# A residual kept in SBUF: selection matmuls in place of scatters in a top-4-of-32 expert layer

## The chip, the core and the metric

The kernel runs on one core of a Trainium2 chip. The metric is the device time of one execution in microseconds. A core has five instruction streams that run beside each other and meet at semaphores: TensorE (PE, matmuls; its weight loads are PEld), VectorE (DVE), ScalarE (ACT), GpSimd (POOL) and SyncE (SP, which here only issues transfers). Sixteen DMA engines move data between HBM (DRAM) and SBUF; matmul results land in PSUM, eight banks of 512 float32 per partition.

## The reference

One decoder block over 512 tokens of width 1024, in float32: a gated recurrence and a dilated attention share one input and one output projection, then a mixture of 32 experts follows, of which each token uses 4.

```python
def _moe(h, router_w, router_b, w_up, b_up, w_down, b_down):
    logits = (h @ router_w + router_b).astype(jnp.float32)
    top_vals, top_idx = lax.top_k(logits, TOP_K)
    gates = jax.nn.softmax(top_vals, axis=-1)
...
    def expert_block(args):
        xb, e = args
        u = xb @ w_up[e] + b_up[e]
        return _clamped_swiglu(u) @ w_down[e] + b_down[e]
...
    return jnp.zeros((N, D), h.dtype).at[sorted_tok].add(y)
```

The block's output is `_rmsnorm(x + _moe(...), final_norm_g)`. The weights of one expert are 8 MiB up (1024 x 2048) and 4 MiB down (1024 x 1024). The 2048 (token, expert) pairs give an expert 64 tokens on average; by the router's logits for these inputs the counts run from 38 to 92.

## The kernel before

**Stages.** The input projection, recurrence and attention take the first 270 us; the output projection and the router run to 307 us. There the rows x (the residual, tile `X`) are complete in SBUF. They are written to the DRAM tensor `residual_rows`, and the normed rows to `normed_rows`. From 318 us the 32 experts follow, one step each, and then the final norm.

**An expert's step.** An expert gets a block of slots, in groups of 32 rows: three groups (96 slots, `BIG`) or two (64 slots, `LESS`). Before the experts start, the kernel ranks them by their counts on the chip, so that the fuller ones get the large blocks; places 0, 1 and the odd ones are `BIG`, 17 in all. Tokens beyond a block go to further blocks at the end, in a loop that tests at run time whether there are any; with these inputs there are none, and each engine only runs through the tests (`TURNS`).

In step p TensorE computes the up products of expert p and the down products of expert p-1. A weight chunk holds 128 rows of w_up or 256 of w_down, 1 MiB; a step has 8 up chunks and 4 down chunks. The stationary operand is a 128x32 piece of the tokens' columns, so four matmuls with different column groups of the array run at a time, each with 512 (up) or 256 (down) moving columns of the float32 weights. Around the chunks stand small things: bias products (L1746, L1764), eight transposes of the next expert's gathered rows (`x_transposed`, L1720), and four or six transposes of the activation output (`a_transposed`, L1728). Each write to PSUM banks 6 and 7 (tile `T`) is copied out by VectorE.

**Weights.** SyncE loads them in pairs of chunks (2 MiB, `load_pair`) into ten buffers in a fixed order; a load waits for `chunk_used`, that is, for the pair that was in its buffer ten pairs before.

**Rows.** GpSimd gathers the next expert's normed rows by an indirect DMA. When the down products of expert q are complete in banks 4 and 5, ScalarE scales one half of the columns by the gates and VectorE the other (`gated`, L783 and L1376, 32x256 pieces) into `y_rows`, and GpSimd scatters these rows with an adding indirect DMA into `residual_rows` (L588). At the end `residual_rows` is read back into SBUF for the final norm (L553).

**Order.** Everything is written out by hand. The steps 2 to 31 are a loop of three rounds with a body of ten steps (`BODY`, L1816), on each engine.

## Time and profile before

| | |
|---|---|
| Time of three runs, median (lowest to highest) | 1394.54 us (1393.95 to 1395.07) |
| The profiled execution | 1393.91 us, its span 1392.1 us |
| TensorE matmuls busy | 1262.6 us, 91% of the span |
| VectorE, ScalarE, GpSimd busy | 400.2, 277.8 and 102.4 us |
| Bytes moved by DMA | 459.38 MB, 330 GB/s over the span |

A row of a timeline gives start and length in us from the span's start, the engine, the line of the kernel, what is written and read, how many instructions are merged, and in brackets the idle time ahead of it and what ended it. A float32 matmul stands as two records, so "x8" on L1754 is four matmuls. Ends of matmuls are modelled and overlap the next; for a price, starts are subtracted.

### The profile page before, as it was taken

The page shows a single profiled execution, that of the slowest core. Times are in us where ns is not written, and L with a number is a line of the kernel's source. Part 1 is how long each engine was busy: PE and PEld are TensorE (multiplying, and loading weights), DVE is VectorE, ACT ScalarE, POOL GpSimd, SP SyncE. Part 2 cuts the span into 40 slices and gives each one's busy share as a digit, 9 for nine tenths or more (in the row PEclk, how much of TensorE's full clock was granted, in tenths as well). Part 3 has the DMA queues.
Part 4 walks back from the last instruction along what each step waited for, and adds up shares of the span by engine and source line. Part 5 has one row for each costly group of instructions (what it writes and reads, how often), then busy time and mean ns, then how long its engine had stood idle before and what let it go on. Part 6 is the DMA issues. An engine that isn't in the chain of part 4 may idle for free.

```text
span 1392.1 us, 31318 instructions
## 1 busy us (share of the span) xinstructions
PE 1262.6 (91%) x13185; PEld 645.4 (46%) x13186; DVE 400.2 (29%) x854; ACT 277.8 (20%) x553; POOL 102.4 (7%) x140
## 2 busy tenths in 40 slices
PE   7999989999999999999898979897989898998990
PEld 6888866684443443433343434343434343333340
DVE  5766745573221122111111111111112121111115
ACT  6455334321111112111111111110101011111112
POOL 0000001000010011000000000001000010100000
PEclk9999999989999999999999999999999999999995
DMA  8422145259999999999999999999999999999943
GB/s 249 135 70 82 46 178 246 92 222 404 361 395 392 402 391 398 393 395 402 403 402 407 402 406 405 402 403 401 403 405 403 396 401 404 398 413 391 414 155 135
DMA packets 71107, 459.38 MB, mean 330 GB/s; under 512 B 7013, under 2 KB 35845, under 8 KB 46304
## 3 DMA queue, kind: packets, MB, share of 16 engines
q1 hardware_dynamic: 64688, 438.52, 78.6%
q0 software_dynamic: 6288, 18.86, 5.8%
q8 instruction: 113, 1.85, 0.5%
q14 instruction: 18, 0.15, 0.0%
HBM read 442.04 MB, written 17.96 MB: 330 GB/s over the span
## 4 chain that ended last, share of the span: by engine, by line
PE 53%; DMA 42%; DVE 3%; issue 1%; ACT 0%; DVEq 0%; SPq 0%
DMA w_raw_pair<-w_down 41%; PE psum L1754 15%; PE psum L1774 15%; PE psum L1496 8%; PE psum L1493 3%; PE psum L1582 2%; PE psum L1720 2%; PE psum L1630 2%; PE psum L1606 1%; PE psum L1746 1%; PE psum L1800 1%; PE psum L1569 1%; PE psum L1647 1%; PE psum L1458 1%; DMA shape_consts<-shape_constants 0%
## 5 line engine op out<-in xcount | busy, mean ns | idle before, releaser
L1754 PE MATMUL psum<-w_raw_pair,x_slots 128*32 128x512 f32 x5184 | 590.8, 608 | 49.9 <-DMA w_raw_pair<-w_up 49.9
L1754 PEld LDWEIGHTS psum<-w_raw_pair,x_slots 128*32 128x32 f32 x5184 | 165.5, 112 | 432.9 <-issue 356.1
L1774 PE MATMUL psum<-w_raw_pair,a_slots 128*32 128x256 f32 x5184 | 294.0, 381 | 9.6 <-DMA w_raw_pair<-w_down 9.5
L1774 PEld LDWEIGHTS psum<-w_raw_pair,a_slots 128*32 128x32 f32 x5184 | 163.7, 110 | 117.5 <-DMA w_raw_pair<-w_down 13.0
L1363 DVE TENSOR_SCALAR lin<-lin 128x768 f32<-128x768 f32 (+1 forms) x32 | 15.9, 498 | 466.7 <-ACT lin L773 466.6
L773 ACT ACTIVATE lin<-psum 128x768 f32<-128x768 f32 (+1 forms) x32 | 22.8, 711 | 600.2 <-PE psum L1754 600.2
L1376 DVE TENSOR_SCALAR y_rows<-psum,gate_t 32x256 f32<-32x256 f32 x162 | 78.5, 484 | 200.5 <-PE psum L1774 198.6
L783 ACT ACTIVATE y_rows<-psum,gate_t 32x256 f32<-32x256 f32 x162 | 75.5, 466 | 300.0 <-PE psum L1774 298.4
L588 POOL DMA_INDIRECT residual_rows<-y_rows,scatter_rows x32 | 46.4, 1450 | 250.8 <-DVE y_rows L1376 231.1
L1496 PE MATMUL psum<-h_low,w_in_high 128*128 128x512 f32 x160 | 63.9, 399 | 0.0
L1496 PE MATMUL psum<-h_high,w_in_high 128*128 128x512 f32 x160 | 62.6, 391 | 0.0
L1496 PE MATMUL psum<-h_high,w_in_low 128*128 128x512 f32 x160 | 62.5, 391 | 0.0
L1357 DVE TENSOR_SCALAR a_slots<-psum 128x768 f32<-128x768 f32 (+1 forms) x32 | 26.6, 833 | 113.5 <-PE psum L1728 112.4
L576 POOL COPY gather_rows<-row_t 96x1 int32 x32 | 5.8, 182 | 665.3 <-PE psum L1720 643.7
L1353 DVE COPY x_slots<-psum 128x768 f32<-128x768 f32 (+1 forms) x32 | 26.4, 825 | 65.1 <-PE psum L1720 53.5
L1720 PEld LDWEIGHTS psum<-shape_consts,gathered 96*128 96x128 f32 (+1 forms) x256 | 33.1, 212 | 13.6 <-issue 13.6
L1720 PE MATMUL psum<-shape_consts,gathered 96*128 96x96 f32 (+1 forms) x256 | 37.9, 289 | 0.0
L1746 PE MATMUL psum<-bias_up_parts,bias_sel_up 96*32 96x512 bf16 x324 | 25.0, 400 | 11.5 <-issue 11.5
L924 DVE TENSOR_TENSOR w_in_low<-w_in_raw,w_in_high 128x1024 fp32r<-128x1024 f32 x24 | 29.3, 1223 | 21.2 <-ACT w_in_high L673 21.2
L580 POOL DMA_INDIRECT gathered<-normed_rows,gather_rows x32 | 32.1, 1004 | 27.8 <-POOL gather_rows L576 27.8
L1728 PEld LDWEIGHTS psum<-shape_consts,glu 128*128 128x128 f32 x162 | 21.9, 208 | 26.4 <-issue 26.4
L1496 PEld LDWEIGHTS psum<-h_low,w_in_high 128*128 128x128 f32 x160 | 30.3, 190 | 7.0 <-issue 0.6
(272 smaller groups left out, 962.4 us busy)
## 6 DMA issues: line engine op xcount, KB each, us to landing
w_raw_pair<-w_up SPq DMA_DIRECT2D x128, 2048.0 KB, 48.2
w_raw_pair<-w_down SPq DMA_DIRECT2D x64, 2048.0 KB, 47.6
w_in_raw<-w_in SPq DMA_DIRECT2D x28, 512.0 KB, 3.8
w_buf<-w_out SPq DMA_DIRECT2D x4, 1024.0 KB, 8.5
x_rows<-x SPq DMA_DIRECT2D x4, 512.0 KB, 5.2
x_rows<-x SPq DMA_DIRECT2D x1, 2048.0 KB, 17.4
residual_rows<-x_rows SPq DMA_DIRECT2D x4, 512.0 KB, 2.8
normed_rows<-h_rows SPq DMA_DIRECT2D x4, 512.0 KB, 2.6
```

What stands on the lines that cost most here:

```text
L580: pool.indirect_dma_start(XG[0:rows, :], None, normed_dram, bass.IndirectOffsetOnAxis(IDXG[0:rows, 0:1], 0), bounds_check=bound, oob_is_er ...
L588: pool.indirect_dma_start(acc_dram, bass.IndirectOffsetOnAxis(IDXS[0:rows, 0:1], 0), Y[0:rows, :], None, compute_op=ALU.add).then_inc(acc_ ...
L783: ins = act.activation(Y[g * STEP:(g + 1) * STEP, j * 256:(j + 1) * 256], Yp2[r, g, :], ACT.Copy, scale=gate_t[r, g, bass.ds(column, 1)])
L924: ins = dve.tensor_tensor(WPL[:, c % 4, :, :], WPR[:, c % 2, :, :], WPH[:, c % 4, :, :].bitcast(F32), ALU.subtract)
L1376: ins = dve.tensor_scalar(Y[g * STEP:(g + 1) * STEP, j * 256:(j + 1) * 256], Yp2[r, g, :], gate_t[r, g, bass.ds(column, 1)], None, ALU.mult)
L1493: ins = pe.matmul(blocks_of(o), h_part[:, k, j * P:(j + 1) * P], w_rows, start=(k == 0 and h_part is HL), stop=(k == DK - 1 and w_part is ...
L1496: ins = pe.matmul(o, w_part[:, j, k, :], h_part[:, k, :], start=(k == 0 and h_part is HL), stop=(k == DK - 1 and w_part is WPL))
L1582: ins = pe.matmul(o, G[:, k, i * P:(i + 1) * P], Wb[:, 0, n % 2, k, :], start=(k == 0), stop=(k == HH - 1))
L1720: ins = pe.transpose(T[:, k, 0:rows], XG[0:rows, at_k:at_k + 2 * P - 1:2], ident[0:rows, 0:rows])
L1746: pe.matmul(U[quarter(j), g, :], BSU[:, :], up_columns(bias_up, j), start=True, stop=False)
L1754: ins = pe.matmul(U[quarter(j), g, :], xs[:, c, quarter(g)], up_columns(w, j), start=False, stop=(c == UPC - 1))
L1774: ins = pe.matmul(Yp2[quarter(j), g, :], As[:, 2 * g + h, quarter(c)], raw[q.slot(m)][:, at_w:at_w + 256], start=False, stop=(c == DNC - 1 ...
```

## The change

The residual is no longer written to DRAM. It stays in the tile `X`, and each expert's rows are added to it there. For expert q: ScalarE writes the gated down products, rounded to float32r, to `YP` (`y_highs`), VectorE writes what the rounding left (`y_lows`), and a 0/1 matrix `SELT` (slot by token) is made by one comparison (`token_sels`). TensorE multiplies it with the two parts in eight pieces of 128 tokens x 512 columns (`move`), and VectorE adds each piece to `X` (`add_moved`). For a `BIG` block a piece takes two float32r matmuls with 96 rows, high and low part; for a `LESS` block both parts stand beneath each other in 128 rows, so one matmul does. The rows of expert q move in step q+2, between the up chunks 3 and 7; those of the last two experts at the end.

The other edits: 16 experts are `BIG` and 16 `LESS`, with places 2, 3 and the last one `LESS`; nine buffers of weights instead of ten (the tenth one's place holds the working tiles); the activation's transposes move from the next step's up chunk 1 to the same step's down chunk 2; steps 2 to 7 are written out, and the loop does five rounds less the first, of six steps each; the planning of further blocks moves from the end into steps 3 to 6 on VectorE; the tests for such blocks are three (`TURNS`) instead of twelve. All scatters, the writing of `residual_rows` and its reading back are gone.

```diff
...
-TURNS = MAXX // 2
+TURNS = ((0, 2), (2, 6), (6, MAXX))
...
-RAW = 20
+RAW = 18
...
-SMALLS = (NE - 2) // 2
+LARGES = (NE - 4) // 2
...
-BODY = 10
+BODY = 6
 ITERS = (NE - 2) // BODY
-OVER_PAIR = 2
+OVER_PAIR = 3
+MOVES = 2 * TT
...
-        pair_at = [hg0, hg0 + 16384, hg0 + 32768, ht0, fk0 + 16384, v0, wb0 + 16384, fk0, wb0, v0 + 16384]
+        pair_at = [hg0, hg0 + 16384, hg0 + 32768, ht0, fk0 + 16384, v0, wb0 + 16384, fk0, wb0]
...
+        xg0 = v0 + 16384
...
+        YP = over("y_parts", [P, 2, D], oa0, F32R)
...
-            return BIG if p < 2 or p % 2 else LESS
+            return BIG if p < 2 or (p > 2 and p % 2 == 0) else LESS
...
-                    freed(sp, "x2", i, n)
-                sp.dma_start(accv[:, i, :], X[:, i, :]).then_inc(S("acc_out"), 16)
                 if i == TT - 1:
+                    full(sp, "x2", TT - 1, 1)
...
-            def scatter(q, col, rows):
...
-            def gated(q, n, column, down_chunks_end):
+            def y_highs(q, n, column, down_chunks_end):
 
                 act.wait_ge(chunk_used, down_chunks_end)
-                act.wait_ge(blocks_added, q + 1)
-                for g in range(n):
-                    for j in range(2):
-                        r = slice(j * STEP, (j + 1) * STEP)
-                        ins = act.activation(Y[g * STEP:(g + 1) * STEP, j * 256:(j + 1) * 256], Yp2[r, g, :], ACT.Copy,
-                                             scale=gate_t[r, g, bass.ds(column, 1)])
-                ins.then_inc(y_ready, 1)
+                if not isinstance(q, int) or q:
+                    act.wait_ge(added, q * MOVES)
+                for half in range(2):
+                    for j in (2 * half, 2 * half + 1):
+                        for g in range(n):
+                            r = quarter(j)
+                            ins = act.activation(YP[quarter(g), 0, j * 256:(j + 1) * 256], Yp2[r, g, :], ACT.Copy,
+                                                 scale=gate_t[r, g, bass.ds(column, 1)])
+                    ins.then_inc(y_high, 1)
...
+            def y_lows(q, n, column):
+
+                for half in range(2):
+                    dve.wait_ge(y_high, q * 2 + (half + 1))
+                    for j in (2 * half, 2 * half + 1):
+                        c = slice(j * 256, (j + 1) * 256)
+                        for g in range(n):
+                            low = YP[quarter(g), 1, c] if n == BIG else YP[quarter(LESS + g), 0, c]
+                            ins = dve.scalar_tensor_tensor(low, Yp2[quarter(j), g, :], gate_t[quarter(g), g, bass.ds(column, 1)],
+                                                           YP[quarter(g), 0, c].bitcast(F32), ALU.mult, ALU.subtract)
+                ins.then_inc(y_low, 1)
+
+            def token_sels(n, column):
+
+                rows, row = (slice(0, BLK), row_f) if n == BIG else (slice(0, P), row_s)
+                dve.tensor_scalar(SELT[rows, :], tokens[rows, :], row[rows, bass.ds(column, 1)], None, ALU.is_equal).then_inc(token_sel, 1)
+
+            def add_moved(q, banks):
+
+                for m in range(MOVES):
+                    x_part = X[:, m // 2, m % 2 * 512:(m % 2 + 1) * 512]
+                    dve.wait_ge(moved, q * MOVES + (m + 1))
+                    dve.tensor_tensor(x_part, x_part, PS[:, banks[m % len(banks)], :], ALU.add).then_inc(added, 1)
...
+                if n_moved is not None:
+                    y_lows(p - 2, n_moved, column_moved)
+                    add_moved(p - 2, MOVE_BANKS)
+                token_sels(n_before, column_before)
                 swiglu(p, n)
                 x_rows(use_x(p + 1), n_next)
-                gated(p - 1, n_before, column_before, q.count(NC))
+                if also is not None:
+                    also()
+                dve.wait_ge(chunk_used, q.count(NC))
+                a_rows(use_a(p), n)
...
+            def move(q, n, m, banks):
+
+                if m == 0:
+                    pe.wait_ge(token_sel, q + 1)
+                    pe.wait_ge(y_low, q + 1)
+                if m >= len(banks):
+                    pe.wait_ge(added, q * MOVES + (m + 1 - len(banks)))
+                pe.sem_inc(S("moves_begun"), 1)
+                o, tok, c = PS[:, banks[m % len(banks)], :], slice(m // 2 * P, (m // 2 + 1) * P), slice(m % 2 * 512, (m % 2 + 1) * 512)
+                if n == BIG:
+                    pe.matmul(o, SELT[0:BLK, tok], YP[0:BLK, 0, c], start=True, stop=False)
+                    ins = pe.matmul(o, SELT[0:BLK, tok], YP[0:BLK, 1, c], start=False, stop=True)
+                else:
+                    ins = pe.matmul(o, SELT[:, tok], YP[:, 0, c], start=True, stop=True)
+                ins.then_inc(moved, 1)
+
+            def moe_step(p, q, n_moved, n_before, n, n_next):
 
                 up_bias(p, n)
                 pe.wait_ge(t_free, use_x(p) + 1)
                 for c in range(UPC):
                     up_chunk(q, c, n)
-                    if c == 1:
-                        a_transposed(p - 1, use_a(p - 1), n_before)
-                if isinstance(p, int):
+                    if n_moved is None:
+                        if c == 1:
+                            a_transposed(p - 1, use_a(p - 1), n_before)
+                    elif 3 <= c < 7:
+                        move(p - 2, n_moved, 2 * c - 6, MOVE_BANKS)
+                        move(p - 2, n_moved, 2 * c - 5, MOVE_BANKS)
+                if n_moved is None:
                     pe.wait_ge(turns_ready, 1)
                     pe.wait_ge(S("turn_gates"), 1)
-                down_bias(p - 1, use_a(p - 1), n_before)
+                down_bias(p - 1, use_a(p - 1), n_before, None if n_moved is None else (added, (p - 1) * MOVES))
                 for c in range(DNC):
                     down_chunk(q, UPC + c, c, n_before)
                     if c == 0:
                         x_transposed(p + 1, use_x(p + 1), n_next)
+                    if c == 2:
+                        a_transposed(p, use_a(p), n)
...
+            for p in range(2, BODY + 2):
+                moe_step(p, step_chunks(p), groups(p - 2), groups(p - 1), groups(p), groups(p + 1))
+            with pe.Fori(1, ITERS) as i:
                 for b in range(BODY):
-                    moe_step(i * BODY + (b + 2), body_chunks(i, b), groups(b + 11), groups(b + 2), groups(b + 3))
-            a_transposed(NE - 1, use_a(NE - 1), groups(NE - 1))
-            down_bias(NE - 1, use_a(NE - 1), groups(NE - 1))
+                    moe_step(i * BODY + (b + 2), body_chunks(i, b), groups(b + 6), groups(b + 7), groups(b + 8), groups(b + 9))
+            pe.wait_ge(u_free, NE)
+            down_bias(NE - 1, use_a(NE - 1), groups(NE - 1), (y_low, NE - 1))
             for c in range(DNC):
+                if c >= 2:
+                    for m in range(4):
+                        move(NE - 2, groups(NE - 2), 4 * (c - 2) + m, LAST_BANKS)
                 down_chunk(END, c, c, groups(NE - 1))
+            for m in range(MOVES):
+                move(NE - 1, groups(NE - 1), m, LAST_BANKS)
...
```

How this stands on TensorE in a step with a `LESS` expert up and a `BIG` one down; `w_raw_pair_n` are the weight buffers, and `y_parts`, `token_sel` the tiles YP and SELT. Before, one such step in the loop body:

```order
L1725 ISA [waits a_ready]
L1728 MATMUL psum<-shape_consts,glu 128x128 [waits t_free]
L1728 MATMUL psum<-shape_consts,glu 128x128 x5
L1754 MATMUL psum<-w_raw_pair_111,x_slots 32x512 [waits raw_landed1]
L1754 MATMUL psum<-w_raw_pair_111,x_slots 32x512 x15
L1754 MATMUL psum<-w_raw_pair_112,x_slots 32x512 [waits raw_landed2]
L1754 MATMUL psum<-w_raw_pair_112,x_slots 32x512 x15
L1754 MATMUL psum<-w_raw_pair_113,x_slots 32x512 [waits raw_landed3]
L1754 MATMUL psum<-w_raw_pair_113,x_slots 32x512 x15
L1758 REGISTER_ALU
L1764 MATMUL psum<-bias_down_parts,bias_sel_down 32x256 [waits y_ready,bsd_ready,t_free]
L1764 MATMUL psum<-bias_down_parts,bias_sel_down 32x256 x11
```

and in the changed kernel, from the up chunk 5 of such a step in the loop:

```order
L1825 MATMUL psum<-y_parts,token_sel 128x512 [waits added]
L1788 MATMUL psum<-w_raw_pair_119,x_slots 32x512 [waits raw_landed7]
L1788 MATMUL psum<-w_raw_pair_119,x_slots 32x512 x7
L1818 REGISTER_ALU
L1825 MATMUL psum<-y_parts,token_sel 128x512 [waits added]
L1818 REGISTER_ALU
L1825 MATMUL psum<-y_parts,token_sel 128x512 [waits added]
L1788 MATMUL psum<-w_raw_pair_119,x_slots 32x512 x8
L1792 REGISTER_ALU
L1795 REGISTER_ALU [waits bsd_ready,t_free]
L1798 MATMUL psum<-bias_down_parts,bias_sel_down 32x256 [waits added]
L1798 MATMUL psum<-bias_down_parts,bias_sel_down 32x256 x11
```

Pieces of the move stand in twos between the up chunks, and the transposes of `glu` are gone from here; the bias products of the down part now wait for `added`, VectorE's last addition.

The end of TensorE's stream, from the last expert's down products on. Before:

```order
L1728 MATMUL psum<-shape_consts,glu 128x128 [waits t_free,a_ready]
L1728 MATMUL psum<-shape_consts,glu 128x128 x5
L1764 MATMUL psum<-bias_down_parts,bias_sel_down 32x256 [waits y_ready,bsd_ready,t_free]
L1764 MATMUL psum<-bias_down_parts,bias_sel_down 32x256 x11
L1774 MATMUL psum<-w_raw_pair_110,a_slots 32x256 [waits raw_landed0]
L1774 MATMUL psum<-w_raw_pair_110,a_slots 32x256 x47
L1774 MATMUL psum<-w_raw_pair_111,a_slots 32x256 [waits raw_landed1]
```

and now:

```order
L1798 MATMUL psum<-bias_down_parts,bias_sel_down 32x256 [waits bsd_ready,y_low,t_free,u_free]
L1798 MATMUL psum<-bias_down_parts,bias_sel_down 32x256 x7
L1808 MATMUL psum<-w_raw_pair_113,a_slots 32x256 [waits raw_landed1]
L1808 MATMUL psum<-w_raw_pair_113,a_slots 32x256 x31
L1822 MATMUL psum<-y_parts,token_sel 128x512 [waits token_sel,y_low]
L1823 MATMUL psum<-y_parts,token_sel 128x512
L1822 MATMUL psum<-y_parts,token_sel 128x512
L1823 MATMUL psum<-y_parts,token_sel 128x512
L1822 MATMUL psum<-y_parts,token_sel 128x512
L1823 MATMUL psum<-y_parts,token_sel 128x512
L1822 MATMUL psum<-y_parts,token_sel 128x512
L1823 MATMUL psum<-y_parts,token_sel 128x512
```

The transposes are gone from this place, the down products wait for the evacuation of expert 30's (`y_low`), and between them stand the matmuls that move expert 30's rows (those of expert 31 follow behind).

## Rows read from the trace of the kernel before

**Rows 1.** The page: a DMA queue; groups as line, out<-in, count, busy, mean ns, idle.

```profile
q0 software_dynamic: 6288, 18.86, 5.8%
...
L1754 PE MATMUL psum<-w_raw_pair,x_slots 128*32 128x512 f32 x5184 | 590.8, 608 | 49.9 <-DMA w_raw_pair<-w_up 49.9
...
L1774 PE MATMUL psum<-w_raw_pair,a_slots 128*32 128x256 f32 x5184 | 294.0, 381 | 9.6 <-DMA w_raw_pair<-w_down 9.5
```

**Rows 2.** Ten steps each: length, PE, PEld, DVE, ACT, POOL, clock, DMA share, GB/s.

```profile
379.26:677.80 298.54, 291.47 (x3534) 124.23 (x3526) 56.82 (x102) 42.44 (x92) 28.38 (x40) 0.99 1.01 398
677.80:1010.40 332.60, 299.36 (x3530) 124.04 (x3530) 53.89 (x90) 41.52 (x90) 28.34 (x40) 0.97 1.01 402
1010.40:1342.30 331.90, 301.24 (x3533) 124.76 (x3530) 53.90 (x90) 41.51 (x90) 28.33 (x40) 0.97 0.99 393
```

**Rows 3.** Timeline of TensorE, steps 1 to 4: start, length, line, count.

```profile
345.00 0.86 PE L1746 MATMUL psum<-bias_up_parts,bias_sel_up 96*32 96x512 bf16 x12
...
371.46 7.98 PE L1774 MATMUL psum<-w_raw_pair,a_slots 128*32 128x256 f32 x144
...
379.26 0.64 PE L1746 MATMUL psum<-bias_up_parts,bias_sel_up 96*32 96x512 bf16 x8
...
379.71 3.62 PE L1754 MATMUL psum<-w_raw_pair,x_slots 128*32 128x512 f32 x32
...
383.26 0.98 PE L1728 MATMUL psum<-shape_consts,glu 128*128 128x128 f32 x6
...
384.18 10.51 PE L1754 MATMUL psum<-w_raw_pair,x_slots 128*32 128x512 f32 x96
...
394.50 0.51 PE L1764 MATMUL psum<-bias_down_parts,bias_sel_down 96*32 96x256 bf16 x12
...
406.46 0.86 PE L1746 MATMUL psum<-bias_up_parts,bias_sel_up 96*32 96x512 bf16 x12
...
412.41 0.75 PE L1728 MATMUL psum<-shape_consts,glu 128*128 128x128 f32 x4
...
413.08 15.66 PE L1754 MATMUL psum<-w_raw_pair,x_slots 128*32 128x512 f32 x144
...
436.93 0.64 PE L1746 MATMUL psum<-bias_up_parts,bias_sel_up 96*32 96x512 bf16 x8
```

**Rows 4.** The same timeline in the second part of the output projection.

```profile
286.71 1.07 PE L1630 MATMUL psum<-w_out_low,attn_T_high 128*128 128x512 f32 x4
287.62 1.07 PE L1630 MATMUL psum<-w_out_high,attn_T_low 128*128 128x512 f32 x4
```

**Rows 5.** Groups by line on VectorE and ScalarE.

```profile
L1376 DVE TENSOR_SCALAR y_rows<-psum,gate_t 32x256 f32<-32x256 f32 x162 | 78.5, 484 | 200.5 <-PE psum L1774 198.6
...
L783 ACT ACTIVATE y_rows<-psum,gate_t 32x256 f32<-32x256 f32 x162 | 75.5, 466 | 300.0 <-PE psum L1774 298.4
...
L1093 DVE TENSOR_TENSOR x_rows<-x_rows,psum 128x512 f32<-128x512 f32 x16 | 11.0, 686 | 24.2 <-PE psum L1582 12.1 <-PE psum L1630 6.3 <-DMA x_rows<-x 3.6
```

**Rows 6.** Timeline of TensorE where steps 12 and 22 begin.

```profile
683.20 1.04 PE L1746 MATMUL psum<-bias_up_parts,bias_sel_up 96*32 96x512 bf16 x8 [5.42 <-issue]
...
684.03 5.47 PE L1754 MATMUL psum<-w_raw_pair,x_slots 128*32 128x512 f32 x32
...
1016.50 1.04 PE L1746 MATMUL psum<-bias_up_parts,bias_sel_up 96*32 96x512 bf16 x8 [6.08 <-issue]
```

**Rows 7.** Timeline of all engines at the end.

```profile
1345.96 12.22 PE L1774 MATMUL psum<-w_raw_pair,a_slots 128*32 128x256 f32 x192
...
1372.44 1.77 SPq L553 DMA_DIRECT2D final_rows<-residual_rows  x4
...
1381.67 0.17 DVE L878 TENSOR_SCALAR small<-small 128x2 f32<-128x2 f32 x1 [9.34 <-issue]
...
1384.21 5.14 SPq L557 DMA_DIRECT2D out<-final_out  x4
...
1386.51 2.48 DVE L1439 SCALAR_TENSOR_TENSOR final_out<-final_rows,small,final_g_rows 128x1024 f32<-128x1024 f32 x2
```

More of the change, by code:

```diff
@@ L609, in _ @@
             gather(3, expert_at(3), use_x(2), groups(3) * STEP)
-            scatter(0, 0, groups(0) * STEP)
-            with pool.Fori(0, ITERS) as i:
+            for p in range(2, BODY + 2):
+                gather(p + 2, expert_at(p + 2), use_x(p + 1), groups(p + 2) * STEP)
+            with pool.Fori(1, ITERS) as i:
                 for b in range(BODY):
                     p = i * BODY + (b + 2)
-                    gather(p + 2, expert_at(p + 2), use_x(p + 1), groups(b + 4) * STEP)
-                    scatter(p - 1, expert_at(p - 1), groups(b + 11) * STEP)
-            scatter(NE - 1, expert_at(NE - 1), groups(NE - 1) * STEP)
+                    gather(p + 2, expert_at(p + 2), use_x(p + 1), groups(b + 10) * STEP)
             pool.wait_ge(S("blocks_known"), 1)
-            nx = pool.value_load(CNT[0:1, 0:1], min_val=0, max_val=TURNS)
-            with pool.Fori(0, TURNS) as turn:
+            nx = pool.value_load(CNT[0:1, 0:1], min_val=0, max_val=len(TURNS))
+            for turn, (first, end) in enumerate(TURNS):
                 with pool.If(nx > turn):
-                    with pool.Fori(0, 2) as half:
-                        j = turn * 2 + half
+                    with pool.Fori(first, end) as j:
                         pool.wait_ge(slot_ready, j + 1)
@@ L829, in _ @@
             act.activation(LG[:, 1, :], LG[:, 1, :], ACT.Exp).then_inc(S("lg_exp"), 1)
-            act.wait_ge(S("acc_out"), 16 * TT)
+            for t in range(TT):
+                act.wait_ge(S(f"normed_out{t}"), 16)
             act.wait_ge(t_full, X0 + 1)
@@ L837, in _ @@
             act.wait_ge(ids_ready, 1)
+            moe_step(1, SECOND, None, groups(1), 0)
             act.wait_ge(S("turn_gates"), 1)
[L839 to L840 removed]
+            for p in range(2, BODY + 2):
+                moe_step(p, step_chunks(p), groups(p - 2), groups(p), expert_at(p - 2))
+            with act.Fori(1, ITERS) as i:
                 for b in range(BODY):
                     p = i * BODY + (b + 2)
[L843 removed]
+                    moe_step(p, body_chunks(i, b), groups(b + 6), groups(b + 8), expert_at(p - 2))
+            y_highs(NE - 2, groups(NE - 2), expert_at(NE - 2), END.count(0))
             bias_row(BSD, of_place(NE - 1), bsd_ready)
[L845 removed]
+            y_highs(NE - 1, groups(NE - 1), expert_at(NE - 1), END.count(DNC))
             act.wait_ge(S("blocks_known"), 1)
[L847 to L848 removed]
+            nx = act.value_load(CNT[0:1, 0:1], min_val=0, max_val=len(TURNS))
+            more = act.value_load(CNT[0:1, 1:2], min_val=0, max_val=MAXX)
+            for turn, (first, end) in enumerate(TURNS):
                 with act.If(nx > turn):
[L850 to L851 removed]
+                    with act.Fori(first, end) as j:
                         act.wait_ge(S("items_ready"), 1)
```

234 lines of the change are left out of this document (112 added, 122 removed).

## The prediction

> **What bounds the kernel now.** I read the stretches of ten steps first. Steps 2 to 11 take 298.5 us, steps 12 to 21 332.6 us and steps 22 to 31 331.9 us, at the same matmul time (291 to 301 us) and with the DMA engines busy all along, at 398, 402 and 393 GB/s [rows 2]. So the weights set the pace of the later two thirds, about 33 us a step, and TensorE that of the first third. The groups by line confirm it: what TensorE waits for in the expert part are the weights, 49.9 + 9.6 us in all [rows 1]. TensorE's reserve is therefore small, and the change puts new work there; its own price per step is the number to get right.
>
> **TensorE's price without waits.** The timeline gives it by starts [rows 3]. Step 1 (96 slots up, 96 down) takes 379.26 - 345.00 = 34.26 us, step 2 (64 up, 96 down) 27.20, step 3 (96 up, 64 down) 30.47. Between 384.18 and 394.50 lie six up chunks for two groups: 10.32 / 12 = 0.86 us for a chunk and group. The down matmuls from 371.46 to 379.26 are 144 records, 72 matmuls: 0.108 us each, or 32 x 0.108 = 3.47 for the four chunks of a group. A pair of steps costs 57.67, a step 28.84 on average, against 33 that the weights take.
>
> **What the weights will take.** The indirect transfers took 5.8% of 1392 us, 80.7 us, for 18.86 MB [rows 1]. The scatters write 81 groups x 32 rows x 4 KB = 10.6 MB of these, by bytes 45 us, at 32 steps 1.4 us a step. Bounds are nothing and all of it, 0 to 2.5 us. The weights' pace becomes 33 - 1.4 = 31.6 us a step (30.5 to 33). Nine buffers instead of ten delay each load by two chunks; over a step of six pairs that still leaves three pairs of reserve, and while TensorE is the slower side it costs nothing.
>
> **The moves on TensorE.** A 128-row float32r matmul of 512 columns follows the last one at (287.62 - 286.71) / 4 = 0.2275 us [rows 4]. A large block needs 8 pieces x 2, a small one 8 x 1. In steps 2 to 31 the experts 0 to 29 move, 15 large and 15 small: 240 + 120 = 360 matmuls, 82 us. To this comes the switch between the 32-column pieces and a full-width matmul. Its nearest rows are the transposes put between up chunks [rows 3]. From 379.71 to 383.26 are 3.55 us for four chunk-groups of 0.86, 0.11 too many. Six transposes take 384.18 - 383.26 = 0.92, four take 413.08 - 412.41 = 0.67: 0.125 for one more and 0.17 fixed. So one insertion costs 0.11 + 0.17 = 0.28 us. A step gets four, each of two pieces: 120 x 0.28 = 34 us. At 512 columns the next weight load may hide better, so the bounds are 0 and 0.56 (both pieces pay); I take 0.28, 116 us in sum, 3.9 a step. With it TensorE's step is 28.84 + 3.85 = 32.7 us, more than the 31.6 of the weights: TensorE becomes the bound.
>
> The Trainium skill says in "TensorE: Matmul & The Clock Gate", section "Back-to-back issue gap", that in a stream of weight loads and matmuls one of 512 columns costs about 131 ns, while an isolated one costs N/2.4 + 2.5 = 216 ns. By the first the 360 matmuls would take 47 us, by the trace 82; the trace agrees with the isolated figure.
>
> **What hides on the other engines.** ScalarE makes the high parts in 12 (large) or 8 (small) pieces of 0.466 us, in two halves; VectorE makes the low parts, which I price at the 0.484 of its present pieces [rows 5]. Large: first half at 2.8 us after the down products, then 12 x 0.484 = 5.8: ready at 8.6 us. The first piece moves behind up chunk 3, at 0.7 + 4 x 3 x 0.86 = 11.0. Small: 1.9 + 3.9 = 5.8 us against 0.45 + 4 x 2 x 0.86 = 7.3. Both fit, by 2.4 and 1.5 us. Each addition into X is a 128x512 one from PSUM, 0.686 us [rows 5], 1.4 for the two pieces of a chunk of at least 1.7 us; the last is hidden by up chunk 7. VectorE goes up by some 10 us per step to about half of it (56.8 us for ten steps now, [rows 2]). The move of the transposes costs nothing: same count, same kind of place. In step 3 the large block of expert 1 is 1.3 us late for a small step; that I leave in the error.
>
> **Other edits.** One large block less: step 3 is now 64 up, 64 down, 27.20 less 3.6 for a down group with its bias and 0.25 for two transposes, 23.4 us. Then 14 pairs follow. The counts after the 14 fullest of the free experts are 62 and 60, under 64, so no further block arises. Writing `residual_rows` and its waits lie beside the router and are not waited for by TensorE; zero.
>
> At the start of steps 12 and 22, the two turns of the loop, TensorE stands still for 5.42 and 6.08 us with nothing that holds it but its own issue, and then takes 5.47 us for four chunk-groups that cost 3.44 at full speed, 2.0 more [rows 6]. Before, the loads went on meanwhile and the time came back. Now there are three turns (after steps 13, 19, 25) and no one gives them back: 3 x 7.75 = 23 us. Bounds: 0 (if the pause shrinks with the transfers' load) and 30.
>
> **The end.** Down products of expert 31 wait for the low parts of expert 30: 8.6 us idle, since no up products lie between any more. Then 7.2 for two groups with bias (2 x 3.6), the moves of expert 30 with 16 x 0.2275 + 2 x 0.28 = 4.2, and 2 us for the slow restart as above: 22.0. From the last down matmul on, before: 1345.96 + 12.22 = 1358.2 to the end at 1392.1, 33.9 us, with the scatter, the read back at 1372.44 and 9.34 us of tests on VectorE for twelve turns [rows 7]. Now: parts 1.9 + 3.9, one piece 0.2, eight additions 5.5, three tests 2.3, half of the norm 1.0 + 2.5, and its last part as before, 1386.51 to 1392.1 with 1.2 ahead of it, 6.8: 24.1 us.
>
> **The sum.** 345.0 + 34.3 + 27.2 + 23.4 + 14 x 57.67 (807.4) = 1237.3; moves 116 and turns 23: 1376.3; end 22.0 + 24.1: 1422.4 us of span. The profiled execution lies 1.8 us above its span and the median of the runs 0.6 above that: 1425 us, 2.2% slower. Put the other way: the gain of 10 us behind the last matmul and of 11 for the one group less pays for a fraction of 116 us of new matmuls, of which the reserve of 60 us waits and their slow restarts takes about half.
>
> **Rivals.**
> Cheap moves. The switches cost nothing since weight loads are pulled ahead, and the turns of the loop shrink to half: 1425 - 34 - 12 = 1379 us, faster. For it: behind waits for weights inside the up chunks nothing is lost (10.32 us for twelve without a gap). Against: both kinds of transposes do lose 0.28. Chance 0.16 with what lies between up to 1391.
> The Trainium skill's page "TensorE: Matmul & The Clock Gate", section "Step-by-step: what each phase is for", says that the queue pulls a weight load ahead of matmuls in flight where row groups do not conflict or the background buffer is free; that is this rival's rule. By it and the 131 ns the time would be 1425 - 34 - 37 = 1354; the rows on transposes speak against it, and it is held in this chance.
> Balance. Switches at half price and turns at a third: 1425 - 17 - 14 = 1394 us, no change. The reserve just pays. Chance 0.04.
> VectorE late. If a low part, which reads two operands, takes 0.8 us instead of 0.484, the first piece of a large block waits for 2.8 + 9.6 = 12.4 us instead of 11.0, of a small one 8.3 instead of 7.3: 15 x 1.4 + 15 x 1.0 = 36 us, 1461 us. It decides from 0.68 us (large) and 0.67 (small). Against it: the addition of four times as many rows and twice the columns takes 0.686. Chance 0.07.
> Forecast as above, TensorE bound at 32.7 us a step: chance 0.73.
>
> **Numbers.** 1425 us; range 1384 to 1447, the low end in the case of cheap moves, the high one with dearer switches (each at 0.45 us adds 20). Within 0.2% (1391.8 to 1397.3) is what a measurement can't tell from no change. Faster 0.16, same 0.04, slower 0.80.
>
> **What would show it.** TensorE's waits for weights almost gone (under 15 us against 59.5), matmul busy share above 94% from 380 us on, the DMA engines no longer busy throughout; pairs of steps near 65.4 us; a group of two pieces of a large block between two up chunks at 1.2 us, of a small one at 0.74; three pauses of 5 to 6 us at loop turns; 8 to 9 us idle ahead of the last down products; 24 us behind the last of them. The prediction is wrong if pairs take under 64 us (cheap moves), if TensorE waits for `y_low` in each step (VectorE late), or if it goes on waiting for weights.

## The result and the profile after

| | median of the runs | range | profiled execution | its span |
|---|---|---|---|---|
| before, in the runs beside the changed kernel | 1394.24 us | 1392.94 to 1395.07 (4) | 1393.91 | 1392.1 |
| changed | 1442.36 us | 1441.18 to 1446.35 (4) | 1442.12 | 1440.3 |

The changed kernel takes 1.0351 times as long, 95% interval 1.0329 to 1.0373: 48 us slower. The forecast was 1425 us.

The page of the changed kernel: the scatters' queue [rows 1], the expert products [rows 1], the chain, the new groups, and the landing of the weights.

```profile
PE 1362.7 (95%) x13431; PEld 691.1 (48%) x13432; DVE 653.6 (45%) x1312; ACT 350.8 (24%) x711; POOL 49.6 (3%) x76
...
q0 software_dynamic: 3152, 8.24, 2.0%
...
PE 93%; DVE 3%; issue 2%; ACT 1%; DMA 1%; DVEq 0%; SPq 0%; ACTq 0%
...
L1788 PE MATMUL psum<-w_raw_pair,x_slots 128*32 128x512 f32 x5120 | 587.1, 600 | 0.0
...
L1808 PE MATMUL psum<-w_raw_pair,a_slots 128*32 128x256 f32 x5120 | 297.3, 382 | 0.0
L1401 DVE TENSOR_TENSOR x_rows<-x_rows,psum 128x512 f32<-128x512 f32 x256 | 164.1, 684 | 263.8 <-PE psum L1823 177.6
...
L1387 DVE SCALAR_TENSOR_TENSOR y_parts<-psum,gate_t,y_parts 32x256 fp32r<-32x256 f32 x320 | 153.6, 480 | 62.1 <-ACT y_parts L773 57.9
...
L1822 PE MATMUL psum<-y_parts,token_sel 96*128 96x512 f32 x128 | 57.0, 445 | 3.7 <-issue 3.7
L1825 PE MATMUL psum<-y_parts,token_sel 128*128 128x512 f32 x128 | 48.1, 462 | 6.2 <-DVE y_parts L1387 6.2
...
L1823 PE MATMUL psum<-y_parts,token_sel 96*128 96x512 f32 x128 | 50.6, 396 | 0.0
...
w_raw_pair<-w_up SPq DMA_DIRECT2D x128, 2048.0 KB, 12.0
```

Read the last column of the two expert lines first. The waits for weights, 49.9 and 9.6 us before, are 0.0 and 0.0. A load of weights that was issued now lands in 12 us, where `w_up` took 48 us before: the queue is no longer full. The chain is TensorE for 93% of the span. Of the new work, TensorE has 384 matmuls in L1822, L1823 and L1825, VectorE 320 low parts and 256 additions.

The stretches, which answer to [rows 2]:

```profile
379.40:677.10 297.70, 293.99 (x3228) 124.60 (x3224) 132.43 (x243) 59.03 (x128) 11.18 (x18) 0.99 0.98 388
677.10:1022.70 345.60, 334.39 (x3654) 139.90 (x3650) 133.04 (x230) 64.78 (x140) 11.60 (x20) 0.99 0.94 374
1022.70:1360.10 337.40, 332.13 (x3654) 141.76 (x3650) 133.04 (x230) 64.80 (x140) 11.60 (x20) 0.99 0.96 382
```

The second and third window hold ten steps each, as before, with two turns of the loop in the second and one in the third; the first holds nine. TensorE is busy for 334 of 346 and 332 of 337 us, where it was 299 of 333 and 301 of 332. VectorE stands at 133 of some 340 us, under half, and the DMA share fell to 0.94 and 0.96.

TensorE's timeline, from step 1 to the third turn of the loop; this answers to [rows 3 and 6]:

```profile
343.76 0.86 PE L1780 MATMUL psum<-bias_up_parts,bias_sel_up 96*32 96x512 bf16 x12
...
350.03 0.98 PE L1765 MATMUL psum<-shape_consts,glu 128*128 128x128 f32 x6 [0.25 <-DVE glu L1376]
...
375.87 0.99 PE L1765 MATMUL psum<-shape_consts,glu 128*128 128x128 f32 x6
...
379.40 0.64 PE L1780 MATMUL psum<-bias_up_parts,bias_sel_up 96*32 96x512 bf16 x8
379.86 7.05 PE L1788 MATMUL psum<-w_raw_pair,x_slots 128*32 128x512 f32 x64
388.78 0.47 PE L1822 MATMUL psum<-y_parts,token_sel 96*128 96x512 f32 x1 [1.87 <-issue]
...
390.19 3.22 PE L1788 MATMUL psum<-w_raw_pair,x_slots 128*32 128x512 f32 x16
...
397.44 1.92 PE L1788 MATMUL psum<-w_raw_pair,x_slots 128*32 128x512 f32 x16
399.30 0.50 PE L1822 MATMUL psum<-y_parts,token_sel 96*128 96x512 f32 x1
...
400.42 1.92 PE L1788 MATMUL psum<-w_raw_pair,x_slots 128*32 128x512 f32 x16
402.16 0.51 PE L1798 MATMUL psum<-bias_down_parts,bias_sel_down 96*32 96x256 bf16 x12
...
414.91 0.64 PE L1780 MATMUL psum<-bias_up_parts,bias_sel_up 96*32 96x512 bf16 x8
...
424.26 0.47 PE L1822 MATMUL psum<-y_parts,token_sel 96*128 96x512 f32 x1 [1.85 <-issue]
...
486.59 0.73 PE L1825 MATMUL psum<-y_parts,token_sel 128*128 128x512 f32 x2
487.26 1.93 PE L1788 MATMUL psum<-w_raw_pair,x_slots 128*32 128x512 f32 x16
489.11 0.73 PE L1825 MATMUL psum<-y_parts,token_sel 128*128 128x512 f32 x2
...
575.41 0.87 PE L1780 MATMUL psum<-bias_up_parts,bias_sel_up 96*32 96x512 bf16 x12
...
611.16 0.64 PE L1780 MATMUL psum<-bias_up_parts,bias_sel_up 96*32 96x512 bf16 x8
...
641.32 0.86 PE L1780 MATMUL psum<-bias_up_parts,bias_sel_up 96*32 96x512 bf16 x12
...
778.83 1.47 PE L1780 MATMUL psum<-bias_up_parts,bias_sel_up 96*32 96x512 bf16 x12 [5.50 <-issue]
...
983.94 1.47 PE L1780 MATMUL psum<-bias_up_parts,bias_sel_up 96*32 96x512 bf16 x12 [5.71 <-issue]
...
1190.28 1.47 PE L1780 MATMUL psum<-bias_up_parts,bias_sel_up 96*32 96x512 bf16 x12 [5.27 <-issue]
```

A piece group of a large block starts at 399.30 and the next chunk at 400.42: 1.12 us for two pieces of two matmuls each. The chunk ahead of it runs from 397.44 to 399.30, 1.86 us, where two chunk-groups of 0.86 would be 1.72. So an insertion costs 1.12 + 0.14 = 1.26 us, of which 4 x 0.2275 are the matmuls and 0.35 the switch. For a small block it is 0.67 (486.59 to 487.26) + 0.13 (1.85 for the chunk, less 1.72) = 0.80, less 0.455 for its two matmuls: 0.34.

At 388.78 and 424.26 TensorE stands 1.87 and 1.85 us ahead of the first large piece of a small step. The profile says "issue", but the low parts on VectorE (L1387) end 0.10 us before each of the two pieces, so `y_low` is what they waited for. In step 2 the chunk at 390.19 then takes 3.22 us instead of 1.9: the granted clock is 0.50 (1.2 GHz) from 390.1 to 392.6. In step 3, after the same wait, it is 1.00 from 424.2 to 428.3 and the next chunk is not slow.

Step 1 has two sets of transposes, its predecessor's at 350.03 and its own at 375.87. From 575.41 to 641.32 lies a pair of steps, 35.75 and 30.16, in sum 65.91 us; the pairs behind it repeat this but for the turns.

### The profile page after: what moved, and what is told of

It is laid out like the page before. It is cut to its first block, busy times and chain, and to the rows that moved or that the text cites. A ratio compares the mean times of both kernels' runs of the same rounds, so it can differ in the third digit from the quotient of the medians.

```text
span 1440.3 us, 32587 instructions
## 1 busy us (share of the span) xinstructions
PE 1362.7 (95%) x13431; PEld 691.1 (48%) x13432; DVE 653.6 (45%) x1312; ACT 350.8 (24%) x711; POOL 49.6 (3%) x76
## 3 DMA queue, kind: packets, MB, share of 16 engines
q0 software_dynamic: 3152, 8.24, 2.0%
## 4 chain that ended last, share of the span: by engine, by line
PE 93%; DVE 3%; issue 2%; ACT 1%; DMA 1%; DVEq 0%; SPq 0%; ACTq 0%
PE psum L1788 39%; PE psum L1808 20%; PE psum L1533 8%; PE psum L1530 3%; PE psum L1822 3%; PE psum L1825 3%; PE psum L1757 2%; PE psum L1823 2%; PE psum L1765 2%; PE psum L1619 2%; PE psum L1667 2%; PE psum L1780 1%; PE psum L1643 1%; PE psum L1606 1%; PE psum L1856 1%
## 5 line engine op out<-in xcount | busy, mean ns | idle before, releaser
L1788 PEld LDWEIGHTS psum<-w_raw_pair,x_slots 128*32 128x32 f32 x5120 | 154.2, 110 | 347.8 <-issue 341.4
L1808 PE MATMUL psum<-w_raw_pair,a_slots 128*32 128x256 f32 x5120 | 297.3, 382 | 0.0
L1401 DVE TENSOR_TENSOR x_rows<-x_rows,psum 128x512 f32<-128x512 f32 x256 | 164.1, 684 | 263.8 <-PE psum L1823 177.6
L773 ACT ACTIVATE y_parts<-psum,gate_t 32x256 fp32r<-32x256 f32 x320 | 149.1, 466 | 324.8 <-PE psum L1808 320.8
L1387 DVE SCALAR_TENSOR_TENSOR y_parts<-psum,gate_t,y_parts 32x256 fp32r<-32x256 f32 x320 | 153.6, 480 | 62.1 <-ACT y_parts L773 57.9
L1367 DVE TENSOR_SCALAR a_slots<-psum 128x768 f32<-128x768 f32 (+1 forms) x32 | 26.4, 825 | 201.1 <-PE psum L1808 200.0
L1822 PE MATMUL psum<-y_parts,token_sel 96*128 96x512 f32 x128 | 57.0, 445 | 3.7 <-issue 3.7
L1825 PE MATMUL psum<-y_parts,token_sel 128*128 128x512 f32 x128 | 48.1, 462 | 6.2 <-DVE y_parts L1387 6.2
L1822 PEld LDWEIGHTS psum<-y_parts,token_sel 96*128 96x128 f32 x128 | 23.9, 187 | 58.1 <-issue 55.3
L1363 DVE COPY x_slots<-psum 128x768 f32<-128x768 f32 (+1 forms) x32 | 26.4, 825 | 53.6 <-PE psum L1757 42.0
L1823 PE MATMUL psum<-y_parts,token_sel 96*128 96x512 f32 x128 | 50.6, 396 | 0.0
L1825 PEld LDWEIGHTS psum<-y_parts,token_sel 128*128 128x128 f32 x128 | 20.2, 195 | 58.4 <-issue 58.2
```

What stands on the lines that cost most here:

```text
L773: ins = act.activation(YP[quarter(g), 0, j * 256:(j + 1) * 256], Yp2[r, g, :], ACT.Copy, scale=gate_t[r, g, bass.ds(column, 1)])
L1387: ins = dve.scalar_tensor_tensor(low, Yp2[quarter(j), g, :], gate_t[quarter(g), g, bass.ds(column, 1)], YP[quarter(g), 0, c].bitcast(F32), ...
L1401: dve.tensor_tensor(x_part, x_part, PS[:, banks[m % len(banks)], :], ALU.add).then_inc(added, 1)
L1788: ins = pe.matmul(U[quarter(j), g, :], xs[:, c, quarter(g)], up_columns(w, j), start=False, stop=(c == UPC - 1))
L1808: ins = pe.matmul(Yp2[quarter(j), g, :], As[:, 2 * g + h, quarter(c)], raw[q.slot(m)][:, at_w:at_w + 256], start=False, stop=(c == DNC - 1 ...
L1822: pe.matmul(o, SELT[0:BLK, tok], YP[0:BLK, 0, c], start=True, stop=False)
```

## The experiments

The runs of the kernel before that stand beside the experiments gave 1392.04, 1391.97 and 1391.69 us in the three sets. Ratios are to these. The changed kernel was not run again beside them: its 1442.36 us belongs to the 1394.24 of the first table, where the kernel before was 2.2 to 2.6 us slower. A difference to 1442.36 is therefore uncertain by about 2 us, and by the ratios it comes out 0.1 to 1.2 us smaller. Within one profile such an offset drops out, so prices are read from pairs of steps as well.

### Moves taken out

```diff
 def move(...):
-    if m == 0:
-        pe.wait_ge(token_sel, q + 1)
-        pe.wait_ge(y_low, q + 1)
...
+    return
 def add_moved(...):
-    for m in range(MOVES):  # wait for moved, tensor_tensor, inc added
+    dve.wait_ge(y_low, q + 1)
+    dve.sem_inc(added, MOVES)
```

> The changed kernel without the selection matmuls and without the additions to the residual; the high and low parts and the selections are still written, and the experts' output is left out. Theory: the moves are all that makes TensorE the bound; without them the weights set the pace again at about 31 us a step, and the time falls to 1320 to 1340 us, with waits for weights back. Rival (nine buffers, the transposes' new place or the evacuation in high and low parts cost time by themselves): above 1350 us. If the weights' pace had not profited from the scatters' absence: about 1380 us.

Measured: 1347.71 us (4 runs), ratio 0.9672 [0.9648, 0.9695]. The experts' output does not reach the residual in it.

```profile
PE psum L1786 <- DMA w_raw_pair<-w_up: 28.8, 22, 2.9
PE psum L1778 <- issue: 15.8, 3, 5.5
PE psum L1796 <- DVE y_parts L1387: 9.2, 1, 9.2
...
PE psum L1806 <- DMA w_raw_pair<-w_down: 8.3, 9, 0.9
```

These are TensorE's waits (total, times, longest). 37.1 us of waits for weights are back, and the time is 95 us below that of the changed kernel. So selection matmuls and switches are what makes it slow: 95 us net. Steps without a wait take 30.71 and 26.96 us, a pair 57.67, as before; with the moves a pair takes 65.91, 8.24 more. The first pair, which moves two small blocks, takes 6.4 more, steps 2 and 3 together 15.5 (65.86 against 50.33), and what lies behind step 31 is 9.8 longer (49.9 against 40.0). With 13 pairs of 8.24 that is a gross price of 139 us. 96 of it stay, counted from step 1 on; 37 fill waits, and the remaining 6 are likely the slow chunks behind such waits, which no run takes apart. The time is 8 us above the top of what was expected, since I thought fewer waits would come back.

### The scatters taken out of the kernel before

```diff
-                pool.indirect_dma_start(acc_dram, ..., Y[0:rows, :], None, compute_op=ALU.add).then_inc(acc_added, 16)
-                pool.wait_ge(acc_added, (q + 1) * 16)
+                pool.sem_inc(acc_added, 16)
```

The read back at the end now waits for the gathers instead.

> The kernel before without the scatter transfers (the experts' output is left out), all else as it was. Theory: the scatters took transfer time that the weights lacked, by bytes 45 us: 1345 to 1352 us, 31.4 us a step where there are waits. Rival (they ran in gaps, or HBM sets the pace): 1385 to 1394 us.

Measured: 1350.19 us (4 runs), ratio 0.9704 [0.9686, 0.9722].

```profile
PE psum L1753 <- DMA w_raw_pair<-w_up: 26.0, 20, 2.4
...
PE psum L1773 <- DMA w_raw_pair<-w_down: 6.8, 8, 0.9
```

The scatters cost the kernel before 42 us, 16 ns for each of their 2592 rows; 27 of the 42 are waits for weights (59.5 less 32.8). By the two profiles all but 2 us of it lies in the steps, not at the end. That is the whole prize of removing them.

The time is close to that of the changed kernel without its moves (1347.7). The 2.5 us between the two are all other edits together once the scatters are gone, and their intervals overlap. So nine buffers, the transposes' new place and the evacuation in two parts do not explain the loss. Singly they were not tested: the end is 8.1 us shorter there (70.6 instead of 78.7 from the last step's start) and the steps are 5.5 us longer, with three turns of the loop instead of two and a second set of transposes in step 1.

The bill, then: scatters -42, other edits -2.5, moves +95, in sum 50 us. That this is the distance from 1392.04 to 1442.36 is arithmetic and no check of its own; side by side the two kernels lie 48 us apart.

### Loops written out

```diff
-            for p in range(2, BODY + 2):
+            for p in range(2, NE):
                 moe_step(p, step_chunks(p), ...)
-            with pe.Fori(1, ITERS) as i:
-                for b in range(BODY):
-                    moe_step(i * BODY + (b + 2), ...)
```

and the same on the other four engines.

> The changed kernel with the steps 2 to 31 written out one after another, no loop. Theory (TensorE bounds the changed kernel, so nothing gives a pause back): the three pauses at the loop's turns (5.3 to 5.7 us each, with the slow matmuls behind them 7 to 9) go, about 23 us less, near 1419 us. Rival (transfers or VectorE set the pace): the pauses were cover for something else, 1435 to 1442 us.

Measured: 1419.09 us (4 runs), ratio 1.0188 [1.0169, 1.0207]: 23.3 us less than with the loop (22.7 by the ratios), as worked out in the prediction (3 x 7.75 = 23). On the timeline of the changed kernel the steps at the three turns are 23.8 us longer than their like.

The same edit on the kernel before:

> The kernel before with the steps 2 to 31 written out. Theory (there the weights set the pace, and the loads run on while TensorE pauses): 0 to 3 us less, 1390 to 1394 us. Rival (a pause costs its time in either kernel): 16 us less, 1377 us.

Measured: 1389.53 us (9 runs), ratio 0.9979 [0.9970, 0.9989]: 2.4 us less. Both results are of the same pause of 5 to 6 us.

```profile
PE psum L1746 <- DMA w_raw_pair<-w_up: 62.5, 37, 3.9
PE psum L1766 <- DMA w_raw_pair<-w_down: 11.9, 13, 2.2
```

In the kernel before written out, the 11.5 us of pauses are gone and the waits for weights have grown from 59.5 to 74.4 us. A pause on an engine that waits for transfers is paid by the transfers, which go on. On the engine that sets the pace nobody pays it.

### One price at a time: fewer insertions, fewer matmuls

Eight pieces in three places instead of four:

```diff
-                    elif 3 <= c < 7:
-                        move(p - 2, n_moved, 2 * c - 6, MOVE_BANKS)
-                        move(p - 2, n_moved, 2 * c - 5, MOVE_BANKS)
+                    elif 3 <= c < 6:
+                        for m in range(3 * c - 9, min(3 * c - 6, MOVES)):
+                            move(p - 2, n_moved, m, MOVE_BANKS)
```

> The changed kernel with the eight pieces of a move in three places (three, three, two, behind the up chunks 3, 4, 5) instead of four places of two. Theory (0.28 to 0.33 us for each change between narrow and full-width matmuls): 30 x 0.3 = 9 us less, near 1433 us. Rival (VectorE's additions then hold a piece back, three banks only): 1440 us or more.

Measured: 1432.72 us (4 runs), ratio 1.0289 [1.0274, 1.0304]: 9.6 us less for 30 insertions less, 0.32 us each (8.6 us and 0.29 by the ratios). On its timeline a pair takes 65.24 us instead of 65.91, with two insertions less: 0.34 each.

A large block moved by its high part alone (its low part is left out of the output):

```diff
-                    pe.matmul(o, SELT[0:BLK, tok], YP[0:BLK, 0, c], start=True, stop=False)
-                    ins = pe.matmul(o, SELT[0:BLK, tok], YP[0:BLK, 1, c], start=False, stop=True)
+                    ins = pe.matmul(o, SELT[0:BLK, tok], YP[0:BLK, 0, c], start=True, stop=True)
```

> The changed kernel without the second matmul of a large block's piece (the low part of large blocks is left out). Theory (a matmul costs 0.23 us in the row): 15 x 8 in the steps and 8 at the end, 128 x 0.23 = 29 us less, near 1413 us. Rival (the matmul itself hides behind the wait for additions or the switch): under 10 us less.

Measured: 1415.92 us (4 runs), ratio 1.0170 [1.0155, 1.0185]: 26.4 us less for 128 matmuls less, 0.21 us each (0.20 by the ratios). By its timeline a pair takes 64.06 instead of 65.91, with eight matmuls less: 0.23 each. Together the pairs give the bill: 360 matmuls and 120 insertions at 0.23 and 0.34 are 83 and 41 us, where the prediction had 82 and 34.

### The rest without the core

The kernel before with its scatters, and everything of the change but its core: 16 large and 16 small blocks, smallest last, blocks planned early, three tests for further blocks; loops written out.

```diff
-TURNS = MAXX // 2
+TURNS = ((0, 2), (2, 6), (6, MAXX))
...
-            return BIG if p < 2 or p % 2 else LESS
+            return BIG if p < 2 or (p > 2 and p % 2 == 0) else LESS
...
+            blocks_in = {3: further_blocks, 4: block_starts, 5: block_offsets, 6: block_values}
```

> The kernel before with all of the change but its core: 16 large and 16 small blocks with the last one small, the planning of further blocks in steps 3 to 6, three tests instead of twelve, steps written out. The scatters and ten buffers stay. Theory: still bound by transfers, the gain is only at the end (last down products 3.5 us shorter, planning and tests some 9 us): 1380 to 1384 us. Rival (the other edits are part of the loss): 1394 us or more.

Measured: 1382.98 us (4 runs), ratio 0.9929 [0.9909, 0.9948]: 9 us faster than before, of which writing out the loops is 2.4 by the run above.

```profile
PE psum L1753 <- DMA w_raw_pair<-w_up: 66.7, 43, 3.9
PE psum L1773 <- DMA w_raw_pair<-w_down: 11.3, 13, 0.9
```

The waits for weights are 78.0 us, against 74.4 in the kernel before with its loops written out. Step 3 is 7.1 us shorter (23.40 instead of 30.47), yet from step 1 to the last one under 2 us of it remain (963.2 against 964.9): the weights set that time. The rest of the gain is at the end: behind the last down matmul it takes 28.2 us instead of the 33.9 of the kernel before (31.9 with its loops written out).

With the scatters also told to skip the slots that hold no token:

```diff
-                                        compute_op=ALU.add).then_inc(acc_added, 16)
+                                        bounds_check=SEQ - 1, oob_is_err=False, compute_op=ALU.add).then_inc(acc_added, 16)
```

> The kernel with all of the change but its core, and with unused slots left out of the scatters by their bound: 512 of 2560 rows. Theory (each scattered row takes transfer time from the weights, 42 us for 2592 rows as measured without scatters): 8 us less than 1383, near 1375 us. Rival (a skipped row costs as much as a written one): 1383 us.

Measured: 1380.14 us (6 runs), ratio 0.9912 [0.9892, 0.9931]. 512 of 2560 rows are left out (the queue moves 16.64 instead of 18.73 MB, 5.1 instead of 5.8%). The intervals of the two kernels overlap: the run does not tell a gain of 3 us from none, and it does speak against 8, which 16 ns for every row would give.

### Half and half

The change treats all blocks alike, but a large block costs TensorE 16 matmuls for 96 slots and a small one 8 for 64. So the small ones go over TensorE and the large ones over scatters, into rows of zeros that are added to the residual once at the end.

```diff
+        BY_PE = [q for q in range(NE) if groups(q) == LESS]
+        BY_DMA = [q for q in range(NE) if q not in BY_PE]
...
+                if isinstance(q, int) and q in BY_DMA:
+                    return            # in move() and add_moved()
...
+                dve.tensor_tensor(X[:, i, :], X[:, i, :], XF[:, i, :], ALU.add).then_inc(S("all_added"), 1)
```

> Both ways in one kernel: the 16 small blocks are moved by TensorE into the residual in SBUF (8 matmuls each, no low pass of its own), the 16 large ones are scattered as before into zeroed DRAM rows that are added at the end. Steps written out, nine buffers. Theory (two budgets: a pair of steps costs TensorE 57.7 + 3.3 = 61.0 us, the transfers some 64.3): weights set the pace at 32.1 us a step, the end costs about 5 us more for the last addition: near 1367 us, below both kernels and below 1383. Rival (moves cost their time wherever they stand): 1400 us.

Measured: 1381.76 us (6 runs), ratio 0.9928 [0.9915, 0.9942], 15 us above what was expected and no faster, by the intervals, than the kernel with all of the change but its core. TensorE waits 27.1 us for `w_up`, 15 times, up to 3.2 us. A pair takes about 65 us instead of 64.3. Step 1 starts at 349.61, where the other profiles have it between 342.67 and 346.52: the rows of zeros are written ahead of the projection's weights, and with them moved, in the second version, it starts at 345.64. The second version writes them later, reads the scattered sums back during the last down products, lets GpSimd add them, and skips slots without a token:

```diff
+                if c == 10:
+                    for t in range(TT):
+                        sp.dma_start(acc_dram[t * P:(t + 1) * P, :], ZR[:, :]).then_inc(S("zeros_out"), 16)
...
+            pool.wait_ge(added, (len(BY_PE) - 1) * MOVES)
+            for i in range(TT):
+                pool.wait_ge(S(f"xf_in{i}"), 16)
+                pool.tensor_tensor(X[:, i, :], X[:, i, :], XF[:, i, :], ALU.add).then_inc(S("all_added"), 1)
```

> The mixed kernel with three repairs: the zero rows are written in a quiet part of the input projection instead of ahead of it; the scattered sums are read back while expert 31's down products run and added by GpSimd instead of VectorE; unused slots are left out of the scatter by its bound (289 of 1536 rows). Theory: 5 us at the start, 6 us at the end, and 289 rows at 42 us / 2592 rows, 5 us: near 1366 us. Rival (GpSimd's additions hold VectorE back, and skipped rows cost as much as written ones): 1375 us or more.

Measured: 1373.95 us (5 runs), ratio 0.9864 [0.9842, 0.9886]. It beats both kernels: 18 us under before, 68 under the changed one. But the moves of the small blocks are only part of that, since loops written out, the other edits and skipped slots came with it: without any move the kernel stands at 1380.14 us (the scatters told to skip, above), and with all blocks moved and loops written out it was 1419.09. So moving the small blocks alone, with its rows of zeros and final addition, is worth 6 us, moving all of them costs some 36 to 39. It misses its own target of 1366 by 8 us. Its waits, and its end:

```profile
PE psum L1834 <- DMA w_raw_pair<-w_up: 27.6, 18, 3.0
...
PE psum L1844 <- DVE y_rows L1420: 4.7, 1, 4.7
```

```profile
1341.91 1.76 SPq L562 DMA_DIRECT2D scattered_in<-scattered_rows  x4
...
1345.43 9.28 POOL L636 TENSOR_TENSOR x_rows<-x_rows,scattered_in 128x1024 f32<-128x1024 f32 x4 [7.78 <-DMA scattered_in<-scattered_rows]
...
1351.46 4.27 PE L1873 MATMUL psum<-y_parts,token_sel 128*128 128x512 f32 x8 [6.27 <-issue]
```

The read back starts at 1341.91, beside the down products, and GpSimd's additions run from 1345.43 beside the last parts. In the first version the additions stood behind the last moves, 4.63 us on VectorE. By the two profiles the start gained 4.0 us of the expected 5 and the part from the last step's start on 3.1 of 6 (72.4 instead of 75.5); the steps between gained 0.3 us (954.2 against 954.5), where the skipped rows were to give 5. The waits for weights did not shrink (27.1 to 27.6 us), though fewer rows were scattered, and no run here says why the weights come no faster.

## Why the prediction was right

The direction, the mechanism and most of the sizes hold; the time was 17 us short, inside the range of 1384 to 1447 but near its upper end: a loss of 31 us was forecast and 48 measured. The price of an insertion and the end were too small, and two things in steps 1 to 3 were left out.

- **TensorE becomes the bound.** Right. Waits for weights 0.0 us where under 15 were forecast, busy 97 to 98% of the later stretches, DMA share below before's. Taking away the matmuls gave 95 us back. The rival of cheap moves is out: it wanted pairs under 64 us, and they take 65.91.
- **Price of a matmul, 0.2275 us.** Right: 0.21 by the run without the low parts, 0.23 by its pairs.
- **Price of an insertion, 0.28 us.** Mis-sized: 0.29 to 0.32 by the times of the run with three places, 0.34 by its pairs, 0.34 and 0.35 on the timeline. It was read from transposes of 128x128. A pair is 0.54 us longer than worked out (65.91 against 65.37, 0.07 for each of eight insertions), over 14 pairs 7.6 us. This is the largest part of the miss, well inside the bounds of 0 and 0.56.
- **Steps 1 to 3.** Mis-sized by about 7 us. I left a late low part "in the error" for step 3 with 1.3 us. In fact steps 2 and 3 both run 64 slots up while a large block moves: TensorE waited 1.87 and 1.85 us, and in step 2 restarted at the lower clock (3.22 us for one chunk). Step 1 took 35.64 us, 1.4 more than before. That is not the moves, as the kernel without them has the same 35.64: "same count, same kind of place" was wrong for the transposes in step 1, which has the old place and the new one.
- **Parts and additions on VectorE and ScalarE hide.** Right. The low part took 480 ns where 484 was taken, the addition 684 for 686. From step 4 on, no piece waits for `y_low` until the end. The rival of a late VectorE is out, but for steps 2 and 3.
- **Loop turns, 23 us.** Right: 5.50, 5.71 and 5.27 us of pause and slow first chunks. Written out, the kernel is 23 us faster.
- **The weights' pace, 1.4 us a step for the scatters.** Right in size: 42 us over 32 steps is 1.3. Where there are waits, the kernel before without scatters takes 31.6 us a step (steps 23 to 30, 62.6 to 63.7 a pair), which is the forecast pace; the kernel before takes 33.1 there.
- **The end.** The wait ahead of the last down products is 9.21 us (8.6 forecast), and from there to the last of them 13.4 as worked out. This answers to [rows 7]. Behind them it takes 27.3 us, not 24.1:

```profile
1399.66 0.62 PE L1798 MATMUL psum<-bias_down_parts,bias_sel_down 96*32 96x256 bf16 x8 [9.21 <-DVE y_parts L1387]
...
1411.11 1.93 PE L1808 MATMUL psum<-w_raw_pair,a_slots 128*32 128x256 f32 x32
...
1413.20 3.83 ACT L773 ACTIVATE y_parts<-psum,gate_t 32x256 fp32r<-32x256 f32 x8 [16.50 <-PE psum L1808]
1415.23 3.96 DVE L1387 SCALAR_TENSOR_TENSOR y_parts<-psum,gate_t,y_parts 32x256 fp32r<-32x256 f32 x8 [2.50 <-ACT y_parts L773]
...
1419.28 4.19 PE L1825 MATMUL psum<-y_parts,token_sel 128*128 128x512 f32 x8 [6.24 <-DVE y_parts L1387]
1420.09 4.87 DVE L1401 TENSOR_TENSOR x_rows<-x_rows,psum 128x512 f32<-128x512 f32 x8 [0.90 <-PE psum L1825]
...
1427.68 0.17 DVE L873 TENSOR_SCALAR small<-small 128x2 f32<-128x2 f32 x1 [2.73 <-issue]
...
1430.22 6.78 SPq L561 DMA_DIRECT2D out<-final_out  x4
...
1432.53 2.48 DVE L1476 SCALAR_TENSOR_TENSOR final_out<-x_rows,small,final_g_rows 128x1024 f32<-128x1024 f32 x2
```

From the last output row computed (1435.01) to the end are 5.3 us, where before it was 3.1; that alone is 2.2 of the 3.2 us. The output transfers land in 4.2 us at the median, before in 2.7. The three tests take 2.73 us (2.3 forecast), the eight moves 4.19.

Summed against the forecast span of 1422.4: start -1.2, step 1 +1.4, steps 2 and 3 +5.7, pairs +7.6, turns +0.8, end and tail +3.8. That is the 18 us to 1440.3. The start is chance: between the profiles of these kernels it moves by up to 4 us.

## What to carry to other kernels

When work is moved from a queue that sets the pace to an engine with reserve, compare its full price there, switches between shapes included, with the waits that engine will still have once the queue is relieved (here 37 us against a gross 139), not with those it has now. Price the two kinds of block apart: with loops written out, moving no block took 1380 to 1383 us, only the half that is cheap on the engine 1374, all of them 1419. Compare a mixed kernel with one that has all edits but the moves, not only with the old one, or it is credited with what the other edits gave. And a pause at a loop's turn that costs little while transfers lag (2.4 us for two) costs its full length (23 us for three) as soon as the pausing engine is the bound.

## What the runs showed of the hardware

- Full-width matmuls put between 32-column ones cost 0.34 to 0.35 us an insertion beyond the 0.2275 us of each matmul, by the timeline of the changed kernel.
- The pause of TensorE at a loop turn does not shrink with the load of the transfers: 5.27 to 5.71 us at 374 to 388 GB/s, 5.42 and 6.08 at about 400. Without the scatters it was 6.3 twice.
- A wait of under 2 us can be followed by a slow chunk, and need not be. After 1.87 us the matmuls at 390.19 took 3.22 us for 16 instead of 1.9, at a granted clock of 0.50; after 1.85 us in step 3, and after the same 1.87 us in the kernel with its loops written out, the clock stayed at 1.00.
- After 6.24 us idle the eight last moves ran at a granted clock of 0.50 (1.2 GHz) and took 4.19 us. They start 0.42 to 0.43 us apart from the second to the sixth, near twice the 0.2275 us of a running TensorE; the last two are 0.56 to 0.6 apart, where each needs a bank that an addition of 0.61 us has to free.
- GpSimd adds one 128x1024 float32 tile in 2.32 us (9.28 for four; the profile's spans on GpSimd are rough); VectorE took 4.63 us for the same four.
- A scattered row of 4 KB costs 16 ns of the kernel's time as long as the weights set the pace, but skipping a fifth of the rows gave 3 us or nothing. Why is open.
